# A two-layer hybrid decoder trunk on one core: triangular inverse in 32x32 products, later bonus sums, masks in pieces, no last state update

## The reference, cut to what matters

```python
def even_mixer(h, w_in, w_out, ...):
    p = h @ w_in
    o_a = rwkv7_mix(p[..., :RWKV_COLS], ...)      # 8 heads x 64
    o_b = gated_deltanet_mix(p[..., RWKV_COLS:], ...)
    return jnp.concatenate([o_a, o_b], axis=-1) @ w_out

# RWKV-7, per token:
sa = jnp.einsum('bhvk,bhk->bhv', S, a_t)
S = S * w_t[:, :, None, :] + sa[..., None] * b_t[:, :, None, :] + v_t[..., None] * k_t[:, :, None, :]
o = jnp.einsum('bhvk,bhk->bhv', S, r_t)
...
bonus = jnp.sum((r_h * k_h * r_k), axis=-1, keepdims=True) * v_h

# gated DeltaNet, per chunk of 64 tokens:
a_mat = jnp.where(strict, (k_beta @ k.T) * decay, 0.0) + jnp.eye(C)
u = tri(a_mat, v * beta[..., None])               # unit lower triangular solve
w = tri(a_mat, k_beta * jnp.exp(g)[..., None])
```

## Time and profile before

| | us |
|---|---|
| three runs | 1550.43, 1552.90, 1553.49; median 1552.9 |
| the profiled execution | 1550.74 |
| its span (first to last instruction) | 1548.3, mean granted clock 0.967 |
| PE busy | 1446.0 (93%) |
| DVE, ACT, POOL busy | 682.0, 605.1, 572.3 |

### The profile page before, as it was taken

The page is one execution under the profiler, slowest core; times in us unless marked ns, Lnnn a source line. Parts: engine busy times, 40 slices in busy tenths (PEclk is TensorE's granted clock), DMA queues, the critical chain, the costliest instruction groups (busy, mean ns, idle before and its releaser), DMA issues.

```text
span 1548.3 us, 24568 instructions
## 1 busy us (share of the span) xinstructions
PE 1446.0 (93%) x10321; PEld 1158.1 (75%) x10321; DVE 682.0 (44%) x1063; ACT 605.1 (39%) x872; POOL 572.3 (37%) x265
## 2 busy tenths in 40 slices
PE   7999899888769999999999799987999999999998
PEld 5787578777758788888888687754467888888886
DVE  4665676777554312213143405877823413132231
ACT  5525463434344423223133335467844313232231
POOL 5343231101023434343434332326944443434441
PEclk9999898999869999999999899998999999999999
DMA  4332110000113232323233222210012232223231
GB/s 141 95 96 68 55 28 3 3 3 3 57 43 95 82 109 82 109 82 106 84 101 90 67 83 69 82 55 1 1 55 83 98 93 93 97 86 104 83 106 55
DMA packets 128392, 110.00 MB, mean 71 GB/s; under 512 B 10678, under 2 KB 126512, under 8 KB 128304
## 3 DMA queue, kind: packets, MB, share of 16 engines
q1 hardware_dynamic: 127712, 107.64, 22.4%
q10 hardware_dynamic: 592, 1.07, 0.2%
HBM read 106.60 MB, written 2.10 MB: 70 GB/s over the span
## 4 chain that ended last, share of the span: by engine, by line
PE 78%; DVE 11%; ACT 5%; issue 3%; POOL 2%; DMA 1%; DVEq 0%; ACTq 0%; SPq 0%; POOLq 0%
PE ps L501 21%; PE ps L506 21%; PE ps L502 21%; PE ps L637 5%; DVE lower L1874 2%; DVE lower L1870 1%; POOL lower L2083 1%; PE ps L652 1%; PE ps L645 1%; PE ps L741 1%; ACT lower L1371 1%; PE ps L614 1%; PE ps L538 1%; PE ps L948 1%; DVE lower L1653 1%
## 5 line engine op out<-in xcount | busy, mean ns | idle before, releaser
L2051 POOL TENSOR_TENSOR w_lo<-lower,w_hi 128x2048 fp32r<-128x2048 f32 x84 | 387.4, 4612 | 637.2 <-ACT w_hi L1027 637.2
L501 PE MATMUL ps<-h_hi,w_hi 128*128 128x512 f32 x792 | 315.9, 399 | 8.9 <-ACT h_hi L1032 5.9
L502 PE MATMUL ps<-h_hi,w_lo 128*128 128x512 f32 x792 | 314.5, 397 | 0.0
L1027 ACT ACTIVATE w_hi<-lower 128x2048 fp32r<-128x2048 f32 x84 | 160.2, 1907 | 242.8 <-PE ps L506 242.8
L506 PE MATMUL ps<-h_lo,w_hi 128*128 128x512 f32 x792 | 201.6, 395 | 0.4
L502 PE MATMUL ps<-a_hi,w_lo 128*128 128x512 f32 x480 | 189.1, 394 | 0.0
L501 PE MATMUL ps<-a_hi,w_hi 128*128 128x512 f32 x480 | 189.1, 394 | 0.0
L501 PEld LDWEIGHTS ps<-h_hi,w_hi 128*128 128x128 f32 x792 | 150.3, 190 | 46.5 <-issue 11.5
L502 PEld LDWEIGHTS ps<-h_hi,w_lo 128*128 128x128 f32 x792 | 150.2, 190 | 36.0 <-issue 0.5
L506 PEld LDWEIGHTS ps<-h_lo,w_hi 128*128 128x128 f32 x792 | 148.7, 188 | 37.4 <-DVE h_lo L1576 1.8
L1819 DVE TENSOR_TENSOR lower<-lower,ps 128x512 f32<-128x512 f32 x64 | 44.0, 687 | 268.7 <-PE ps L506 268.7
(11 more groups left out here) (356 smaller groups left out, 1992.4 us busy)
## 6 DMA issues: line engine op xcount, KB each, us to landing
lower<-in_mlp_w_dram SPq DMA_DIRECT2D x64, 1024.0 KB, 5.4
lower<-in_ev_w_in_dram SPq DMA_DIRECT2D x30, 512.0 KB, 3.8
lower<-in_od_w_in_dram SPq DMA_DIRECT2D x10, 1024.0 KB, 5.0
lower<-in_ev_w_out_dram SPq DMA_DIRECT2D x4, 1024.0 KB, 5.1
lower<-in_od_w_out_dram SPq DMA_DIRECT2D x4, 1024.0 KB, 5.1
out_dram<-lower SPq DMA_DIRECT2D x4, 512.0 KB, 3.2
lower<-in_od_w_in_dram SPq DMA_DIRECT2D x6, 256.0 KB, 3.8
upper<-in_x_dram SPq DMA_DIRECT2D x1, 1024.0 KB, 7.8
```

Source lines behind the costliest of these rows:

```text
L501: pe.matmul(o, wh, xh, start=(i_ == 0), stop=False)
L502: pe.matmul(o, wl, xh, start=False, stop=False)
L1027: act.activation(WH[:, u % 2, :, 0:w], RAW[:, u % 2, :, 0:w], ACT.Copy).then_inc(hi_ready, 1)
L2051: pool.tensor_tensor(WL[:, u % 2, :, 0:w], RAW[:, u % 2, :, 0:w], as_f32(WH[:, u % 2, :, 0:w]), ALU.subtract)\
```

## The change

Four edits. (1) `below_blocks` and `joined_blocks` go through a new function `quarters`. Up to level 3 it multiplies only the four 32x32 blocks on the diagonal of the 128x64 operand pairs (32 products a group instead of 16); at level 4 only the one off-diagonal 32x32 block of each chunk that MERGE takes (16 products a group), and the second product there multiplies the matrices in their lower positions. What DVE does not take from the banks is no longer computed. (2) In `plan` and in the lists of PE and DVE the gq sums come before the first GV tile, the bonus sums behind it; GV is split into GV0 and GV1. (3) GpSimd makes the low parts of tiles 3, 4 and 5 at three places among the masks. (4) In the pass behind the last chunk PE leaves out the state sums, DVE the decay and sum of the state; `chunk_out` gets the two waits that stood in `state_sums`. No weight, load or operation elsewhere is changed.

```diff
--- before.py
+++ after.py
@@ -304,8 +304,8 @@
         Q0 = 71
         plan = (("par0", 1, 0), ("x", 8, 0), ("lora0", 1, 0), ("lora1", 1, 0), ("norm", 1, 1), ("par1", 1, 0),
                 ("ab", 1, 0), ("K0", 1, 0), ("abt", 1, 0), ("K1", 3, 0), ("wa", 8, 1), ("g", 4, 1), ("R", 4, 0),
-                ("V", 4, 0), ("cum", 1, 1), ("GQ", 4, 0), ("kk", 4, 1), ("GK", 4, 0), ("bon", 4, 0),
-                ("gq", 4, 1), ("GV", 4, 0), ("gk", 4, 1), ("Z", 4, 0))
+                ("V", 4, 0), ("cum", 1, 1), ("GQ", 4, 0), ("kk", 4, 1), ("GK", 4, 0), ("gq", 4, 1),
+                ("GV0", 1, 0), ("bon", 4, 0), ("GV1", 3, 0), ("gk", 4, 1), ("Z", 4, 0))
         pq, readers = {}, []
         for name_, n_, by_ in plan:
             pq[name_] = len(readers)
@@ -318,8 +318,10 @@
         tiles = [("lora0", 0, 1536, P), ("lora1", 0, 1664, P), ("ab", 0, GDN_BA, 16), ("K0", 0, 512, P)]
         tiles += [("K1", c, 640 + c * P, P) for c in range(3)]
-        tiles += [(n_, c, o_ + c * P, P) for n_, o_ in (("R", 0), ("V", 1024), ("GQ", GDN_QKV), ("GK", GDN_QKV + 512),
-                                                       ("GV", GDN_QKV + 1024), ("Z", GDN_Z)) for c in range(4)]
+        tiles += [(n_, c, o_ + c * P, P) for n_, o_ in (("R", 0), ("V", 1024), ("GQ", GDN_QKV), ("GK", GDN_QKV + 512))
+              for c in range(4)]
+        tiles += [("GV0", 0, GDN_QKV + 1024, P)] + [("GV1", c, GDN_QKV + 1152 + c * P, P) for c in range(3)]
+        tiles += [("Z", c, GDN_Z + c * P, P) for c in range(4)]
         tile_q = [pq[n_] + c for n_, c, _, _ in tiles]
         q_out, q_m1, q_m2 = [71, 214], [80, 223], [88, 231]
@@ -593,11 +595,12 @@
             head_sums0("kk", SQ_KK)
             for u in range(19, 23):
                 tile(u)
+            pe.wait_ge(sq_grp, 2)
+            head_sums0("gq", SQ_GQ)
+            tile(23)
             pe.wait_ge(bonus_in, 4)
             head_sums0("bon", [BON[:, c, :] for c in range(4)])
-            pe.wait_ge(sq_grp, 2)
-            head_sums0("gq", SQ_GQ)
-            for u in range(23, 27):
+            for u in range(24, 27):
                 tile(u)
             pe.wait_ge(sq_grp, 3)
             head_sums0("gk", SQ_GK)
@@ -692,12 +695,30 @@
                 pe.wait_ge(r_kd, s + 1)
                 both_halves(2, MK, VR[s % 2], True).then_inc(f_mkv, 1)
+            def quarters(b, lev, mats, vals, lower):
+
+                for h_ in range(NH):
+                    j, q = h_ // 2, h_ % 2
+                    for i in range(4):
+                        here_ = i // 2 * 2
+                        if lev < LAST - 1:
+                            row, col, m_, n_ = i, i, i % 2, i % 2
+                        elif i % 2 == 0:
+                            row, col, m_, n_ = (here_, here_ + 1, 1, 0) if lower else (here_ + 1, here_, 0, 1)
+                        else:
+                            continue
+                        rows, cols = (slice(x * 32, x * 32 + 32) for x in (row, col))
+                        mm = pe.matmul(ps[cols, b, h_ * HD + n_ * 32:h_ * HD + n_ * 32 + 32],
+                                       mats[rows, j, q, m_ * 32:m_ * 32 + 32], vals[rows, j, q, n_ * 32:n_ * 32 + 32],
+                                       start=True, stop=True)
+                return mm
+
             def below_blocks(s, lev):
                 n = 2 * LAST * s + 2 * lev
                 for g, (lt, ti) in enumerate(((LTR, TIR), (LTG, TIG))):
                     pe.wait_ge(inv_t, n + (2 if lev == 0 else g + 1))
-                    both_halves(g, lt, ti, True).then_inc(inv_x, 1)
+                    quarters(g, lev, lt, ti, True).then_inc(inv_x, 1)
             def joined_blocks(s, lev):
                 n = 2 * LAST * s + 2 * lev
@@ -708,9 +729,9 @@
                     else:
                         pe.wait_ge(inv_q, 2 * (LAST - 1) * s + 2 * (lev - 1) + g + 1)
                     if lev < LAST - 1:
-                        both_halves(g, qi[s % 2], xm, True).then_inc(inv_y, 1)
+                        quarters(g, lev, qi[s % 2], xm, True).then_inc(inv_y, 1)
                     else:
-                        both_halves(g, xm, qi[s % 2], True).then_inc(inv_y, 1)
+                        quarters(g, lev, xm, qi[s % 2], False).then_inc(inv_y, 1)
             def state_reads(s, k):
                 c = 2 * s + k
@@ -750,6 +771,8 @@
                 outer(5, KGT[s % 2], VN, True).then_inc(f_sg, 1)
             def chunk_out(s):
+                pe.wait_ge(r_u, 2 * s + 2)
+                pe.wait_ge(r_y, 2 * s + 2)
                 both_halves(6, RK[s], VR[s % 2], True)
                 both_halves(6, RBM[s], UN, False).then_inc(f_or, 1)
                 both_halves(7, GRK[s], VN, True).then_inc(f_og, 1)
@@ -784,8 +807,9 @@
                 if ahead:
                     below_blocks(s, 0)
                     joined_blocks(s, 0)
+                if behind and ahead:
+                    state_sums(m, 1)
                 if behind:
-                    state_sums(m, 1)
                     chunk_out(m)
                 if ahead:
                     for lev in range(1, LAST - 1):
@@ -796,7 +820,7 @@
                     turned_out(m)
                 if ahead:
                     joined_blocks(s, LAST - 1)
-            pe.wait_ge(e_state, 2 * TT + 1)
+            pe.wait_ge(e_state, 2 * TT)
             pe.wait_ge(r_tr, TT)
             pe.wait_ge(r_tg, TT)
             pe.wait_ge(bank_read, Q0)
@@ -1054,7 +1078,7 @@
                 last.then_inc(sq_grp, 1)
             def silu0(i):
-                act.wait_ge(p_read[0], p_reads(pq[("GQ", "GK", "GV")[i // 4]] + i % 4))
+                act.wait_ge(p_read[0], p_reads(tile_q[15 + i]))
                 act.activation(GQKV[:, i, :], GQKV[:, i, :], ACT.Silu).then_inc(conv_used, 1)
             tile_hi(0)
@@ -1540,15 +1564,15 @@
                     t.step(dve.tensor_tensor(wide(B), wide(KK), wide(B), mul))
                     dve.wait_ge(l0_act, 1)
                     dve.tensor_tensor(wide(EREST), wide(EREST), wide(BETA), mul)
+            convolved("GV0", 0, 8)
             for c in range(4):
                 q = pq["bon"] + c
                 dve.tensor_tensor(BON[:, c, :], filled0(q), V[:, c, :], mul).then_inc(p_read[0], 1)
-            for c in range(4):
-                convolved("GV", c, 8 + c)
-                if c == 0:
-                    dve.wait_ge(rs_grp, 2)
-                    dve.scalar_tensor_tensor(out=wide(GQ), in0=wide(GQ), scalar=float(HD) ** -0.5,
-                                             in1=wide(Z), op0=mul, op1=mul)
+            dve.wait_ge(rs_grp, 2)
+            dve.scalar_tensor_tensor(out=wide(GQ), in0=wide(GQ), scalar=float(HD) ** -0.5,
+                                     in1=wide(Z), op0=mul, op1=mul)
+            for c in range(3):
+                convolved("GV1", c, 9 + c)
             dve.wait_ge(rs_grp, 3)
             for c in range(4):
                 ins = dve.tensor_tensor(GK[:, c, :], GK[:, c, :], SQ_GK[c], mul)
@@ -1743,11 +1767,11 @@
                     state_reads(m, 1)
                 if ahead:
                     first_inverse(s)
-                if behind:
+                if behind and ahead:
                     solved(m, 1)
                 if ahead:
                     joined_blocks(s, 0)
-                if behind:
+                if behind and ahead:
                     state_sums(m, 1)
                 if ahead:
                     joined_blocks(s, 1)
@@ -1986,10 +2010,13 @@
                 t.link(pool.memset(HEADS2[p * HD:(p + 1) * HD, p * HD:(p + 1) * HD], 1.0))
             t.link(pool.memset(SCANM.rearrange("p (k t) -> p k t", k=NC)[:, :, 0:1], 0.0))
+            tile_lo(3)
             first = FULL[:, 0, :].rearrange("p (n q) -> p n q", q=2)[:, :, 1]
             t.link(pool.memset(first, -1.0))
             select(first, 0, [[-2, P // 2]], 1, 0.0, ALU.is_equal)
             for lev in range(1, LEVELS):
+                if lev == 3:
+                    tile_lo(4)
                 b = 1 << lev
                 last = int(lev == LEVELS - 1)
                 low = FULL[:, lev, :].rearrange("p (n q w) -> p n q w", q=2, w=b)[:, :, last, :]
@@ -1997,6 +2024,7 @@
                 select(low, 0 if last else -b, [[-2 * b, P // (2 * b)], [0, b]], 1, 0.0)
                 select(low, b - 1 if last else 2 * b - 1, [[2 * b, P // (2 * b)], [0, b]], -1, 0.0)
+            tile_lo(5)
             for g in range(16):
                 col = (g % 2) * NH + g // 2
@@ -2027,7 +2055,7 @@
                 pool.tensor_tensor(b, b, EDN[:, :, :, 1:CW], mul)
                 pool.tensor_tensor(k, k, EDN[:, :, :, 1:CW], mul).then_inc(e_kb, 1)
-            for u in range(3, len(tiles)):
+            for u in range(6, len(tiles)):
                 tile_lo(u)
             pool.wait_ge(l0_dve, 1)
```

## The result

| | before | changed |
|---|---|---|
| runs beside each other, median | 1552.8 us | 1592.6 us (1590.0 to 1596.3, 4 runs) |
| ratio, 95% interval | 1 | 1.0268 (1.0239 to 1.0296): 41.6 us slower |
| profiled execution | 1550.74 | 1596.31 |
| its span, mean granted clock | 1548.3, 0.967 | 1594.4, 0.928 |

The forecast of 1539.0 was wrong in sign, and the result lies outside its range. The profiled execution of the changed kernel is the slowest of its four, so its span is 46.1 us over that of before and the stages add up to more than 41.6. Where the time went is plain from a table of stages, in us. The first column is where PE begins the transposes of pass 0, the second runs from there to the same point of pass 1, the third from there to the first DVE operation of `mixed` in pass 3 (the inverse is done), the fourth on to the last of these operations behind the last chunk.

A forecast was written before the change was run, and what follows sets the result against it. Inverse levels were taken as bound by both PE time and handovers. Terms -10.0 (inverse), -2.2 (masks), -1.2 (bonus), -0.5 (tail) sum to -13.9, 1550.7 to 1536.8, plus 2.2 to the median: 1539.0 us, range 1529 to 1551.

The forecast's parts named there:

- Nothing from the levels: Rival, chance 0.20: instruction blocks or DVE handovers keep an inverse level at 3.85 us; only 3.9 us gained, 1549.0.
- The slow rival: Inverse: every matmul record has a floor near 27 ns whatever its size, giving 1589.7 us; chance 0.10.
- the four starts in 0.02 us: 64x128 products on four tiles started 7 ns apart, taken as evidence against a 27 ns floor per record.
- The 32x32 group and the chain of a level: Inverse: 64 records in 0.50 us, a level in 3.05 us, 0.8 less; the inverse -10.0 in all.
- The clock: Passes: 2.5 us charged for products at half clock; as a rival, PE stays at 1.2 GHz, 1563, chance 0.07.
- The switches of tile: Inverse: some twelve switches between 64 and 32 wide tiles at under 0.1 us each, 1.0 us charged.
- Masks: GpSimd's masks made in pieces, so PE's tile 3 starts near 32.7 instead of 34.92: -2.2 us.
- Bonus sums: Bonus sums behind the first v tile, ending near 178, the fourth waiting for ACT until about 177.0: -1.2 us.
- Tail: No state update behind the last chunk; DVE's first output operation stretched to about 3 us by GpSimd's split: -0.5 us.

The follow-up runs named there:

- e13: e2 with the 64x64 products of levels 1 to 3 as a loop of three trips on PE: 1550.5 us, ratio 1.0005.
- e3: The changed kernel with levels 1 to 3 as a loop of three trips on PE, same 32x32 products: 1569.1 us, ratio 1.0132.
- e4: The changed kernel with half the products at levels 0 to 3 (second diagonal block of each chunk left out, inverse incomplete): 1550.7 us, ratio 0.9995.
- e14: e2 with level 4 alone in 32x32 products, number of instructions unchanged: 1556.1 us, ratio 1.0044.
- e2: The changed kernel with the inverse back in 64x64 products, the masks, bonus sums and tail changes kept: 1542.8 us, ratio 0.9948.
- e10: e3 with level 0 back in 64x64 products, one block of instructions less a pass: 1557.7 us, ratio 1.0049.
- e7: The kernel before with only the state update behind the last chunk left out: 1550.6 us, ratio 1.0001.
- e9: e2 with each 64x64 product of levels 0 to 3 issued as two of 32 columns: 1618.3 us, ratio 1.0437.
- e8: e2 with DVE's first output product (QSS times EG) moved ahead of its waits for PE's outputs: 1542.8 us, ratio 0.9953.

## Why the prediction was wrong

**The step that failed** is the bound on instruction supply, in the rival "Nothing from the levels": "a level now takes two blocks of PE instructions instead of one ...; if they can't come every 1.5 us, ... the level stays at 3.85". The right number of blocks stood there, with the wrong ceiling. The time of a level whose two blocks can't come in 1.5 us is not the old one but twice the time of a block, and 3.5 us each gives 7. The trace of before had a bound that I didn't use. A block in 3.85 us is the rate of its pass 0; the fastest 128 records of its passes take 3.62 us (from 280.79), and its closest packets begin 3.49 us apart. Nothing showed that blocks can come faster, so the slow end was 7.0 to 7.7 us a level, where the changed kernel took 7.45. I read the spacing as PE's demand alone. It was that (e13), but the supply's ceiling lay only 10% above it.

**The slow rival** gave 1589.7, near the 1592.6, by a sum that holds for another reason: 128 records in 3.5 us are 27 ns each, whether each has that floor or a block of them does. What I held against the floor, the four starts in 0.02 us, was right: e3 has 9.4 ns a record. That its price came out near the result is luck; I ruled out the mechanism and took the price out with it.

**The 32x32 group and the chain of a level** were about right where the instructions were there: a level of 3.20 us in e3 for a forecast of 3.05, a group of 64 records in 0.60 for 0.50.

**The clock** was charged with 2.5 us. Small products cost more than that even without more instructions: 7.3 us in e4, 14.9 in e14 against e2. This rival was right in kind; its 1563 was never met alone. Of the 50 us between e2 and the changed kernel, 21 by the ratios went with the loop and 13 with one more block less. Of the last 16, e10 shows 8.7 us as idle time put down to issue, with the two blocks of the loop's first trip; how the rest divides between the clock and the loop is not settled. **The switches of tile**, charged with 1.0, had no row behind them; in e14 one costs no more than 0.05 us (0.15 for 0.10).

**Masks**: -2.2 forecast, -1.6 measured (-3.1 to 0.2), with the idle time falling from 2.40 to 0.41 (tile 3 at 33.36, forecast 32.7). **Bonus sums**: -1.2 forecast, -2.2 measured. The fourth sum waited for ACT as said, to 176.23 (forecast 177.0). **Tail**: -0.5 forecast, +0.2 measured in e7 (-1.4 to 1.7), and DVE's first output operation was stretched, as forecast in kind, to 4.70 us for about 3. Together they gave 8.1, not 3.9, and part of that is where the clock happened to fall.

## What to carry to other kernels

Count the instructions of an unrolled stretch before cutting its products smaller: where the trace shows a rate only by demand (one block in 3.5 to 3.85 us), its closest spacing is the bound for the slow end, and twice the instructions is twice that time. Making an engine's work smaller can be a loss where other work shares its clock (e14); look at the granted clock of the whole stage. And when a gap moves instead of closing, look at what stands first in the queue of the engine that PE waits for: moving one DVE product behind four convolutions gave 8.4 us, as much as the three good edits together.

## What the runs showed of the hardware

- PE's instructions came in blocks of 16 KB, one in about 3.5 us though a packet took 1.1, with PE idle 1.2 to 2.0 us ahead of most when it used one up sooner. A loop body of two blocks was not fetched again on later trips (34 packets for 50), and a trip cost 0.24 us beside unrolled code, the loop's own semaphore and waits included.
- Two-record fp32 products of 32x32 on four tiles in turn ran at 9.4 ns a record; 64x64 weights with 32 columns cost as much a record as with 64 (53 and 54 ns from start to start at half clock).
- The granted clock did not go with PE's busy time: in e9 it was 0.50 where PE was busy for 60.14 of 61.00 us, and 0.99 where it was busy for 169.23 of 183.00 with the same kinds of product.
- A change from 64x64 to 32x32 weights cost no more than 0.05 us (0.15 us from start to start in e14, 0.10 at the same place in e2 without the change).
- A DVE operation with two inputs in SBUF stood still while GpSimd's split ran (4.70 us for 0.69), and so did a product of 8 columns with a constant (2.14 for 0.17), while two operations with one input in PSUM took their usual 0.69 beside it and a reduction its usual 0.67 (e8).
